# Layers unrolled, weights laid out in equal slabs, and column norms in a two-layer hybrid decoder block

## What is computed

```python
mod = silu(c) @ W_ada + b_ada          # 1024 -> 6 x 1024: shift1, scale1, gate1, shift2, scale2, gate2
h = RMSNorm(x) * (1 + scale1) + shift1
proj = h @ w_in                        # 3152 columns for the mixers, 3 x 1024 gate logits
#   A: latent attention (w_uq, w_ukv, 8 heads)   B: block attention (4 heads)
#   C: indexer-selected attention, top 64 keys (4 heads)
merged = sum_i sigmoid(g_i) * (y_i @ w_br_i)
x = x + gate1 * (merged @ w_out)
x = x + gate2 * SwiGLU(RMSNorm(x) * (1 + scale2) + shift2)   # w_gu 1024 x 5632, w_down 2816 x 1024
```

## Time and profile before

| | us |
|---|---|
| median of 3 runs (lowest, highest) | 1064.75 (1064.21, 1068.41) |
| span of the profiled execution | 1062.6 |
| PE busy | 956.0 |
| DVE busy | 719.5 |
| ACT busy | 485.5 |
| DMA moved | 206.57 MB, 194 GB/s over the span |

### The profile page before, as it was taken

How to read it: one execution, slowest core, us unless ns; L and a number is a source line. 1 busy time by engine, 2 the same in 40 slices (tenths; PEclk the granted TensorE clock), 3 DMA queues, 4 the chain that set the end, 5 groups by cost and what they waited for, 6 DMA issues and landing times.

```text
span 1062.6 us, 18513 instructions
## 1 busy us (share of the span) xinstructions
PE 956.0 (90%) x6874; PEld 903.1 (85%) x6874; DVE 719.5 (68%) x984; ACT 485.5 (46%) x656; POOL 41.7 (4%) x61
## 2 busy tenths in 40 slices
PE   1499798999997899999969979899999889999996
PEld 1299787987797899999969978798779789999995
DVE  5577678967686657667648767896768665766661
ACT  2353388635524543434335438753552453343431
POOL 2100000000100000000010000000010000000000
PEclk9999999999999899999999999999999989999998
DMA  8578854351257268787445985344125716778731
GB/s 333 214 261 318 295 176 120 119 159 41 80 198 278 58 221 274 263 291 259 159 167 194 333 297 169 120 121 158 41 80 195 281 53 225 265 269 289 257 106 40
DMA packets 116010, 206.57 MB, mean 194 GB/s; under 512 B 6088, under 2 KB 92264, under 8 KB 110824
## 3 DMA queue, kind: packets, MB, share of 16 engines
q1 hardware_dynamic: 108704, 154.75, 43.3%
q0 software_dynamic: 6912, 50.33, 13.0%
q10 hardware_dynamic: 328, 0.61, 0.2%
HBM read 204.64 MB, written 1.05 MB: 194 GB/s over the span
## 4 chain that ended last, share of the span: by engine, by line
PE 58%; DVE 15%; DMA 12%; ACT 7%; issue 6%; SPq 1%; ACTq 0%; DVEq 0%
PE bank L566 16%; PE bank L567 15%; PE bank L568 15%; DMA raw<-in_w_in_dram 8%; DVE w_lo L1162 4%; ACT w_hi L908 3%; DMA front<-in_w_ada_dram 2%; DMA raw<-in_w_gu_dram 2%; DVE acc L1403 1%; PE bank L632 1%; PE bank L634 1%; PE bank L633 1%; PE bank L584 1%; DVE acc L1201 1%; ACT acc L1063 1%
## 5 line engine op out<-in xcount | busy, mean ns | idle before, releaser
L1162 DVE TENSOR_TENSOR w_lo<-raw,w_hi 128x2048 fp32r<-128x2048 f32 (+2 forms) x162 | 315.7, 1962 | 142.6 <-ACT w_hi L908 139.9
L566 PE MATMUL bank<-h_hi,w_hi 128*128 128x256 f32 x1216 | 350.7, 288 | 13.0 <-DVE h_lo L1187 9.8
L908 ACT ACTIVATE w_hi<-raw 128x2048 fp32r<-128x2048 f32 (+2 forms) x162 | 265.6, 1648 | 211.5 <-PE bank L568 114.5
L567 PE MATMUL bank<-h_lo,w_hi 128*128 128x256 f32 x1216 | 347.0, 285 | 0.0
L568 PE MATMUL bank<-h_hi,w_lo 128*128 128x256 f32 x1216 | 346.7, 285 | 0.0
L566 PEld LDWEIGHTS bank<-h_hi,w_hi 128*128 128x128 f32 x1216 | 236.1, 194 | 19.3 <-issue 15.5
L567 PEld LDWEIGHTS bank<-h_lo,w_hi 128*128 128x128 f32 x1216 | 236.2, 194 | 0.1
L568 PEld LDWEIGHTS bank<-h_hi,w_lo 128*128 128x128 f32 x1216 | 236.0, 194 | 0.0
L566 PE MATMUL bank<-y_hi,w_hi 128*128 128x256 f32 x480 | 135.5, 282 | 0.0
L567 PE MATMUL bank<-y_lo,w_hi 128*128 128x256 f32 x480 | 135.2, 282 | 0.0
L568 PE MATMUL bank<-y_hi,w_lo 128*128 128x256 f32 x480 | 135.0, 281 | 0.0
(11 more groups left out here) (179 smaller groups left out, 1053.3 us busy)
## 6 DMA issues: line engine op xcount, KB each, us to landing
raw<-in_w_gu_dram SPq DMA_DIRECT2D x88, 512.0 KB, 5.1
front<-in_w_ada_dram POOLq DMA_DIRECT2D x16, 1536.0 KB, 7.0
raw<-in_w_in_dram SPq DMA_DIRECT2D x24, 1024.0 KB, 5.8
raw<-in_w_down_dram SPq DMA_DIRECT2D x22, 1024.0 KB, 7.0
raw<-in_w_in_dram SPq DMA_DIRECT2D x32, 591.0 KB, 5.8
front<-in_w_ada_dram POOLq DMA_DIRECT2D x16, 1024.0 KB, 6.4
front<-in_w_ada_dram SPq DMA_DIRECT2D x8, 1024.0 KB, 7.4
raw<-in_w_out_dram SPq DMA_DIRECT2D x8, 1024.0 KB, 5.1
```

The lines of the kernel that those rows point to most:

```text
L566: nc.tensor.matmul(b_out, st_hi, mv_hi, start=start, stop=False, skip_group_check=True)
L567: nc.tensor.matmul(b_out, st_hi, mv_lo, start=False, stop=False, skip_group_check=True)
L908: nc.scalar.activation(w_hi[:, slot, 0:n], raw[:, slot, 0:n], ACT.Copy).then_inc(hi_ready.sem, 1)
L1162: nc.vector.tensor_tensor(w_lo[:, slot, 0:n], raw[:, slot, 0:n], w_hi[:, slot, 0:n], ALU.subtract)\
```

## The change

All loops are unrolled: layers, chunks and feed-forward pairs are straight code, waits compare with constants, and `apart` is gone. The host lays all weights out as slabs in the order of use, one contiguous run of up to 8 KB per partition and one transfer per slab; x and the result are held in DRAM by channels, so TensorE no longer transposes them; bias and gain vectors come as columns.

The input projection is k-outer: in pass A the columns from 1104 on (2048) go into all eight banks, one slab for each of the eight contraction tiles (`S_A`); in pass B the first 1104 columns go into six banks as 368 each (`S_B`). The query-latent transposes come behind the first gate slab.

w_ada is held transposed, and a tile is two columns of `mod` (2048 words per partition). VectorE multiplies each half by silu(c), broadcast to all partitions, and sums along the row in one instruction (`ada_sum`). Eight tiles come in the start-up, taking turns with the first eight slabs; the others in the order `ADA_SEQ`, loaded by GpSimd into two buffers: four beside pass B, then in layer 0 eight between the branches and the second norm (`ada_next(2)` twice, `ada_next(4)`) and twenty beside the feed-forward, in layer 1 four beside pass B and four beside the feed-forward.

A norm sums one column at a time: the squares are the stationary operand and one column of ones the moving one, for 128 tokens each (`norm_sum`), so the sum stands as a column; square root and reciprocal run on 128x2, the result is broadcast and transposed (`norm_spread`) to all partitions. The sums for the first tiles stand between the last matmuls of the product before, and the x_t updates wait for single output tiles (`xo_done`, `xd_done`) instead of the slab. Activation tables are loaded ahead of use.

```diff
+ADA = [(SH1 + c, SC1 + c) for c in range(KT)] + [(G1 + c, G1 + c + 1) for c in range(0, KT, 2)] \
+    + [(SH2 + c, SC2 + c) for c in range(KT)] + [(G2 + c, G2 + c + 1) for c in range(0, KT, 2)]
+A_P, A_B, A_W, A_F = 0, 8, 12, 20
+N_ADA = len(ADA)
+ADA_B = [(0, A_B + i) for i in range(4)]
+ADA_W = [(0, A_W + i) for i in range(8)]
+ADA_F = [(0, A_F + i) for i in range(4)] + [(1, A_P + i) for i in range(8)] + [(1, A_W + i) for i in range(8)]
+ADA_B1 = [(1, A_B + i) for i in range(4)]
+ADA_F1 = [(1, A_F + i) for i in range(4)]
+ADA_SEQ = ADA_B + ADA_W + ADA_F + ADA_B1 + ADA_F1
...
+            def load(l, s):
+                n = l * NS + s
+                if n >= RING:
+                    sp.wait_ge(lo_ready.sem, n - RING + 1)
+                w = slab_words(s)
+                sp.dma_start(raw[:, n % RING, 0:w], slabs[l, s, :, 0:w]).then_inc(raw_in[n % RING].sem, 16)
...
+            sp.dma_start(x_t[:, :, :].rearrange("p a t -> p (a t)"), x).then_inc(x_in.sem, 16)
+            load_ada_pro(0)
+            load(0, 0)
+            load_ada_pro(1)
+            load(0, 1)
+            load_ada_pro(2)
...
+            def load_ada(n):
+                pool.wait_ge(ada_used.sem, KT + n - 1 if n > 1 else KT)
+                l, tile = ADA_SEQ[n]
+                pool.dma_start(ada_raw[n % 2], ada[l, tile]).then_inc(ada_in[n % 2].sem, 16)
+            n = 0
+            for l in range(DEPTH):
+                for _ in range(4):
+                    load_ada(n)
+                    n += 1
+                pool.wait_ge(scored.sem, scored.at(l, NH))
+                for _ in range(len(ADA_W) + len(ADA_F) if l == 0 else len(ADA_F1)):
+                    load_ada(n)
+                    n += 1
...
+            def norm_sum(l, which, k):
+                pe.wait_ge(sq_done.sem, sq_done.at(l, 8 * which + k + 1))
+                b = bank[NORM_BANKS[which][0]]
+                for t in range(TT):
+                    last = nc.tensor.matmul(b[:, t:t + 1], norm_sq[k % 4][:, t * P:(t + 1) * P], ones[:, 0:1],
+                                            start=(k == 0 and t == 0), stop=(k == KT - 1), skip_group_check=True)
                 last.then_inc(ss_done.sem, 1)
...
+            for l in range(DEPTH):
+                if l == 0:
+                    for k in range(KT):
+                        norm_sum(0, 0, k)
+                norm_spread(l, 0)
+                pe.wait_ge(rstd_done.sem, rstd_done.at(l, 1))
+                for k in range(KT):
+                    slot = slab(l, S_A + k)
+                    pe.wait_ge(hlo_done.sem, hlo_done.at(l, k + 1))
                     for t in range(TT):
...
+                        hh, hl = h_hi[:, k, t * P:(t + 1) * P], h_lo[:, k, t * P:(t + 1) * P]
+                        for cc in range(4):
+                            wh, wl = w_hi[:, slot, 512 * cc:512 * (cc + 1)], w_lo[:, slot, 512 * cc:512 * (cc + 1)]
+                            o = bank[4 * t + cc][:, :]
+                            nc.tensor.matmul(o, hh, wh, start=(k == 0), stop=False)
+                            nc.tensor.matmul(o, hl, wh, start=False, stop=False)
+                            last = nc.tensor.matmul(o, hh, wl, start=False, stop=(k == KT - 1))
+                            if k == KT - 1 and 4 * t + cc < 7:
+                                last.then_inc(pa_done.sem, 1)
...
+                            if k == 0:
+                                pe.wait_ge(chunk_out.sem, chunk_out.at(l, 3 * t + cc + 1))
...
+                        if m == 3:
+                            last.then_inc(slab_used.sem, 1)
+                        elif kh and m == 1:
+                            last.then_inc(xo_done.sem, 1)
+                        if o == 3 and m in (1, 2):
+                            if m == 1:
+                                pe.wait_ge(m_done.sem, m_done.at(l, 4))
+                            norm_sum(l, 1, 2 * m - 2)
+                            norm_sum(l, 1, 2 * m - 1)
+                for k in range(4, KT):
+                    norm_sum(l, 1, k)
+                norm_spread(l, 1)
...
+                    for m in range(KT):
+                        last = channel_tile(slot, bank[m // 2][:, (m % 2) * T:(m % 2 + 1) * T], m * P, [0, D], hi, lo,
+                                            m % 2 == 0, i == 0, i == FG - 1)
+                        if i == FG - 1 and m < KT - 1:
+                            if m % 2:
+                                last.then_inc(xd_done.sem, 1)
+                            if l + 1 < DEPTH and m >= 3:
+                                norm_sum(l + 1, 0, m - 3)
+                    last.then_inc(slab_used.sem, 1)
...
+            def norm_squares(l, which):
+                table(ACT.Sqrt)
+                for k in range(KT):
+                    if which:
+                        act.wait_ge(x_done.sem, x_done.at(l, k + 1))
+                    elif l:
+                        act.wait_ge(x_done.sem, x_done.at(l - 1, 8 + k + 1))
+                    elif k == 0:
+                        act.wait_ge(x_in.sem, 16)
+                    if k >= 4:
+                        act.wait_ge(ss_done.sem, ss_done.at(l, 8 * which + k - 3))
+                    nc.scalar.activation(norm_sq[k % 4], x_t[:, k, :], ACT.Square).then_inc(sq_done.sem, 1)
...
+            def ada_sum(place, l, tile):
+                for e, col in enumerate(ADA[tile]):
+                    w = place[:, D * e:D * (e + 1)]
+                    ins = nc.vector.tensor_tensor_reduce(w, w, cond[:], 1.0, cols[:, l, col:col + 1], ALU.mult, ALU.add,
+                                                         mod[:, l, col:col + 1])
+                ins.then_inc(ada_used.sem, 1)
+            state = {"ada": 0}
+            def ada_next(count=1):
+                for _ in range(count):
+                    n = state["ada"]
+                    dve.wait_ge(ada_in[n % 2].sem, 16 * (n // 2 + 1))
+                    ada_sum(ada_raw[n % 2], *ADA_SEQ[n])
+                    state["ada"] = n + 1
...
+            for l in range(DEPTH):
+                if l == 0:
+                    for k in range(KT):
+                        dve.wait_ge(apro_in[k].sem, 16)
+                        ada_sum(ada_pro[k % 7], 0, A_P + k)
+                        scale_coef(0, 0, k, 1)
+                        if k == 0:
+                            dve.sem_inc(coef_done.sem, 1)
+                            norm_rs(0, 0)
+                        norm_scaled(0, 0, k)
+                        if k != 1:
+                            lo(0, S_A + max(k - 1, 0))
+                        norm_lo(0, 0, k)
+                    lo(0, S_A + KT - 1)
+                else:
+                    norm_rs(l, 0)
+                    norm_tiles(l, 0)
...
                     banks = BR_BANKS[hf]
                     for m in range(2):
                         lo(l, S_BR + 2 + 2 * hf + m)
+                    if l == 0:
+                        ada_next(2)
...
+                if l == 0:
+                    ada_next(4)
+                scale_coef(l, 1, 0, KT)
+                lo(l, S_FF)
+                for k in range(KT):
+                    if k == 4:
+                        lo(l, S_FF + 1)
+                    if k % 4 == 0:
+                        dve.wait_ge(xo_done.sem, xo_done.at(l, k // 4 + 1))
+                    elif k % 4 == 2:
+                        dve.wait_ge(slab_used.sem, slab_used.at(l, S_OUT + 3 + k // 4))
+                    nc.vector.scalar_tensor_tensor(out=x_t[:, k, :],
+                                                   in0=bank[(6, 0)[k // 4] + k % 4 // 2][:, (k % 2) * T:(k % 2 + 1) * T],
+                                                   scalar=mod[:, l, G1 + k:G1 + k + 1], in1=x_t[:, k, :], op0=ALU.mult,
+                                                   op1=ALU.add).then_inc(x_done.sem, 1)
+                norm_rs(l, 1)
+                norm_tiles(l, 1)
+                def glu_step(i):
+                    par = i % 2
...
+                def ada_step(i):
+                    if l == 0:
+                        ada_next(2 if i < FG - 1 else 0)
+                    elif 2 <= i < 6:
+                        ada_next()
...
+                if l + 1 < DEPTH:
+                    scale_coef(l + 1, 0, 0, KT)
+                    for k in range(2):
+                        lo(l + 1, S_A + k)
                 for k in range(KT):
+                    if k < KT - 2 and k % 2 == 0:
+                        dve.wait_ge(xd_done.sem, xd_done.at(l, k // 2 + 1))
+                    elif k == KT - 2:
+                        dve.wait_ge(slab_used.sem, slab_used.at(l, NS))
                     nc.vector.scalar_tensor_tensor(out=x_t[:, k, :], in0=bank[k // 2][:, (k % 2) * T:(k % 2 + 1) * T],
-                                                   scalar=mod_a[:, k:k + 1], in1=x_t[:, k, :], op0=ALU.mult,
+                                                   scalar=mod[:, l, G2 + k:G2 + k + 1], in1=x_t[:, k, :], op0=ALU.mult,
```

983 lines of the change are left out of this document (445 added, 538 removed).

## The result

| | before | after |
|---|---|---|
| median us (lowest, highest) | 1064.48 (1061.42, 1068.41) | 1010.31 (1007.47, 1010.87) |
| span of the profiled execution | 1062.6 | 1008.2 |
| PE / DVE / ACT busy, us | 956.0 / 719.5 / 485.5 | 934.6 / 695.9 / 474.8 |
| DMA moved, MB | 206.57 | 198.83 |

The account below looks back on a forecast made before the run. TensorE, 99% busy, was taken to bound the feed-forward; gains lay elsewhere. Start-up with layer 0's projection 95.5, middles 225.9 and 205.3, feed-forwards 191.9 and 190.3, layer change 5.9, layer 1's projection 71.3, end 3.6, plus 2.1: 991.7 us, range 958 to 1036.

Parts of the forecast that it names:

- The price of the new sum: VectorE's multiply-and-sum over 1024 words of w_ada: 1.31 us, 2.62 us per tile, with bounds 2.1 and 4.75 a tile.
- Rival (b): New sum at half rate: +17 us at the start, +17 at the eight tiles, about +10 in layer 0's feed-forward: 1036; chance 0.10.
- Layer 0's middle: 225.9 us against layer 1's 205.3: eight w_ada tiles in VectorE's queue give +17 us in place of -4.6.
- Rival (d): Whole kernel: unrolled instructions each come from memory once, adding 107 us, slower than before: 1099 us; chance 0.04.
- Rival (a): Layer 0's middle: the eight tiles hide after all where VectorE waits for ScalarE: 970 us; chance 0.14.
- with 1 us for the reciprocal: Start-up: first tile lands at about 11 us, plus 1 us, then VectorE's steps of 6.1; last remainder ends at 61.9.
- + 1.2 (norm sums) + 0.4: Layer 0's feed-forward: these additions to 188.6 us of matmuls and 1.7 of half clock give 191.9 us.
- 1.2 us a norm: Second norm and layer 0's feed-forward: charge for norm sums put between dense matmuls.
- The price of 0.4: Norm chain: a pair of one-column sums on TensorE takes 0.4 us, between 0.1 and 0.7.
- What goes are the waits for slabs: Layer 1's projection: 82.0 us become 71.3, upper bound 80, with 4.2 MB of w_ada tiles beside it where 12.6 moved.
- Rival (c): Projections: the three-slot ring starves the shorter slabs, two waits of 5 us in each: 1012 us; chance 0.20.
- 1.7 us of loss: Feed-forward: half clock at the start costs 1.7 us beside 188.6 of matmuls, giving 190.3 in layer 1.

Follow-up runs that it names:

- e3: Changed kernel without the eight sums of w_ada tiles between branches and second norm of layer 0, loads and waits kept: 996.89 us, ratio 0.9357.
- e7: e2_sums_behind with layer 0's eight w_ada tiles loaded earlier and summed apart from each other, no sum left out: 977.97 us, ratio 0.9170.
- e2_sums_behind: e1 with all sixteen one-column sums of the norms between layers and ahead of the feed-forward behind the product's last matmul: 994.29 us, ratio 0.9345.
- e4: Changed kernel with the start-up's norm earlier: four squares ahead of silu(c), square-root table behind the squares, sums not waiting for constants: 1005.56 us, ratio 0.9432.
- e9: e7 with the start-up of e4 and slab k's remainder in step k of VectorE's start-up pipeline, not k+1: 971.08 us, ratio 0.9103.
- e1: Changed kernel with the remainders of layer 1's slabs 0 and 1 behind the x_t updates, not ahead of them: 1003.64 us, ratio 0.9425.
- e10: Changed kernel with 8.4 MB more moved beside layer 1's projection, w_ada tiles loaded again that nobody reads: 1011.05 us, ratio 0.9496.
- e6: Changed kernel with each slab's transfer made of eight runs of 1 KB per partition (552 B in pass B): 1012.93 us, ratio 0.9489.
- e12: Changed kernel with both 8.4 MB more beside layer 1's projection and slabs in eight short runs: 1011.44 us, ratio 0.9500.
- e11_rs_first: e9 with the norm's reciprocal ahead of slab 0's remainder in VectorE's start-up queue: 969.21 us, ratio 0.9102.

## Why the prediction was right, and where it was off

**Right.** The price of the new sum: 1.280 us, with the read of the accumulator overlapped into a distance of 1.21 between starts; forecast 1.31. Rival (b), a sum at half rate, falls: two f32 sources in SBUF with an accumulator took (1.280 - 0.164)/1024 = 1.09 ns a word. The rule of the Trainium skill (Vector Engine (DVE) Microarchitecture Reference, Points that are easy to get wrong) that stood beside that rival doesn't show in this instruction. VectorE's step in the start-up took 5.72 us (6.1). Pass B took 25.0 (25.2), layer 1's projection 71.1 (71.3), its middle 205.1 (205.3), the end 3.5 (3.6). Layer 0's middle is 22.8 us longer than layer 1's (forecast 20.6), with the waits that were named, at the merge and at the x_t updates; e3 and e7 show that the eight tiles are the cause. In part the size is luck: around the second norm layer 0 waits 14 us more than layer 1, and 5 us are the lower clock behind the longest wait, for which the forecast had no term. Rival (d), code from memory, falls: 337 starts in 40 us where the earlier trace rows has 336. Rival (a) falls with e3. The prediction read a clock of 0.79 at the kernel's end where the earlier trace rows has 0.77; nothing in its sum rests on the difference. No run undoes one part of the change by itself (the transposed w_ada, the equal slabs, the norms by columns, the straight code), so how the 54 us divide among the parts is read from the stretches and not shown.

**Start-up, +4.9: the step "with 1 us for the reciprocal".** The forecast had the norm ready when VectorE was. The sums begin only at 14.13 us: silu(c) stands ahead of the squares and waits for c until 10.18, and TensorE's wait for the constants stands ahead of the sums (in e2_sums_behind that one is listed last, 14.3 us). They take 6.96 us, and VectorE waits 7.35. What it lost it won back in part by the shorter step: its last remainder ended at 66.9 in place of 61.9, TensorE began pass B at 75.6 in place of 70.2. The forecast's 61.9 was itself 1 us too late, since eight steps of which one has no remainder are 7.6 steps and not 7.8. e4 and e9 show the cause: with the sums earlier, the first matmul and the end of pass A move with them.

**Layer 0's feed-forward, +8.7: the term "+ 1.2 (norm sums) + 0.4".** This is the largest miss. The diff shows `lo(l + 1, S_A + k)` ahead of the updates that the sums wait for; the prediction listed who stands in VectorE's queue at the second norm and didn't do the same here. Of the 8.7 us, 2.4 are the wait, 2.3 the half slab at the lower clock, 1.7 the four pairs of sums (3.3 in place of the term's 1.6), and 2.4 are the same as in layer 1's feed-forward. e1 takes 6.7 us back by that order alone.

**The sums, 1.2 us a norm.** A pair (two matmuls) has four records, and eight pairs take 3.6 us at full clock (e2: 32 records behind the product) and 6.96 in the start-up: 0.45 and 0.87 a pair. The price of 0.4 with bounds of 0.1 to 0.7 was right for the one and too low for the other. But the other seven pairs of a norm were put at 1.2 us together, which is less than seven times the prediction's own 0.4; at 0.45 they are 3.2. (Only four of them stand between matmuls in this kernel, the other three behind.) It was charged as if dense work covered them, and TensorE can't cover its own work.

**Layer 1's projection, right for a wrong reason.** "What goes are the waits for slabs" is what happened, but the reason given, four tiles in place of 12.6 MB beside it, falls: with 8.4 MB more (e10), with short runs (e6), with both (e12) the 71.1 us stay within 0.3. What did take the waits away stays open. Layer 0's own pass A could have told, moving 289 GB/s with one early wait of 2.4 us.

**Rival (c)** gave 1012 us and lies nearer to the result than the forecast does. That is chance: TensorE waited for no slab behind the second in either projection, and the 18.6 us lie in other places.

**Layer 1's feed-forward, +2.4.** The lower clock lasts 5.5 us behind the norm (26 matmuls 0.21 apart) where 1.7 us of loss were counted and 2.5 came; 0.8 more is a wait ahead of the last down slab, which the forecast didn't have, and 0.8 the pace, 0.1195 us a matmul where 0.119 was taken.

## What to carry to other kernels

When a step is moved under other work, ask what that other work's engine is: sums put between matmuls aren't hidden on a full TensorE, they only tie the matmuls behind them to two more engines (e2). Ahead of each wait that is put into a dense stretch, write down the whole queue of the engine that answers it, in every place where the pattern occurs; the miss here was the second place. Work that must get done somewhere costs what its place costs: eight tiles, each with 2.5 us of sums, made layer 0 25 us longer than layer 1 in a row (e2) and 5 us spread (e7).

## What the runs showed of the hardware beyond expectation

- An f32 matmul with one moving column and 128x128 f32 weights shows two records, which start 0.112 us apart at full clock and 0.213 in the start-up (where the clock's column reads 1.00, though this is the distance seen elsewhere at 0.50). So it takes 0.22 us, nearly twice as long as a 256-column matmul of the products (0.119).
- What a pause of TensorE costs beyond itself: behind 2.4 us (last down slab) and 9.8 us (second norm of layer 0) the granted clock was 0.50 for the next 20 us, from 520.7 to 541.1 and from 312.5 to 332.9, with the 256-column matmuls 0.21 us apart; the pauses of the norm's own chain fall into both stretches. Behind 1.2 us (second norm of layer 1) it stayed at 1.00. The difference between 11.8 and 6.5 us for the same 56 records is that. It isn't fixed by the pause alone: behind the same wait of 2.8 us ahead of the pair transposes (L602) it was 1.00 in layer 0 and 0.53 in layer 1 of one execution, and the sixteen transposes took 1.97 us and 3.60.
- A change of ScalarE's table took 1.28 us and nothing more: silu(c) ends at 11.24, the load starts at 11.25, the next operation at 12.55. The Trainium skill (ScalarE: Activation LUTs, What ACT_TABLE_LOAD costs) adds a drain of 1.38 us, which this trace doesn't show.
- In e11_rs_first the start-up moved 425 GB/s over 20 us:

```profile
20.00:40.00 20.00, 19.45 (x74) 15.88 (x75) 19.77 (x29) 8.63 (x7) 0.00 (x0) 1.00 1.01 425
```

That is 45 GB/s more than the 380 that the prediction took from the earlier trace rows. The Trainium skill (Perfetto Trace Analysis, Roofline) puts the ceiling of one active core at about 435 GB/s by its 16 DMA engines; a share of 1.01 at 425 agrees.
